# A forget gate in two passes, its norm amid the query product, and low key parts written once: one change to a two-block fp32 model kernel

## The chip, the cores and the metric

The kernel runs on one core of a Trainium2 chip. The metric is the device time of one execution in microseconds.

## What is computed

Two model blocks, one after the other, on 512 tokens of width 1024 in fp32. The first block has a gated linear recurrent layer and a "fox" attention layer; the second has two hybrid layers (short convolution, retention, MLP). The change lies in the fox layer, cut here to what matters:

```python
def rms_norm(x, g):
    y = xf * lax.rsqrt(jnp.mean(xf * xf, axis=-1, keepdims=True) + EPS)
    return (y * g.astype(jnp.float32)).astype(x.dtype)

def fox_mixer(h, w_in, b_f, w_out):          # 16 heads of 64
    u = h @ w_in
    q, k, v, gate = four times 1024 columns of u
    f_logit = u[..., 4 * FOX_WIDTH:] + b_f   # the last 16 columns, one for each head
    cum = jnp.cumsum(jax.nn.log_sigmoid(f_logit), axis=1)
    ...
        logits = jnp.einsum("bqhd,bkhd->bhqk", q_blk, kf) * scale
        logits = logits + (cq_blk[..., :, None] - ck[:, :, None, :])   # from cum
        logits = jnp.where(mask, logits, NEG_INF)
        p = jax.nn.softmax(logits, axis=-1)
        return jnp.einsum("bhqk,bkhd->bqhd", p, vf)
    ...
    return (o * jax.nn.silu(gate)) @ w_out
```

## The kernel before

Everything lies transposed, features on the 128 partitions and the 512 tokens on the free axis: `x` is 8 tiles of 128x512. TensorE multiplies in fp32r, a rounded fp32, and accuracy is had by splitting every operand into a rounded high part and a low part that holds the remainder. A product is three passes: high weights times high activations, high times low, low times high. The weights come from memory in chunks of 128x1024 (two tiles of 128x512). `w_raw`, `w_hi` and `w_lo` are rings of four chunks. For each chunk, three ahead of its use, ScalarE rounds `w_raw` to `w_hi` (`round_ahead`, L1271), VectorE subtracts to make `w_lo` (`remainder`, L1894), and TensorE waits for `lo_ready` before it uses the chunk.

The eight PSUM banks form two sets of four; products take them in turn ("turns"). A full product of four chunks is 96 matmuls: for each of 8 tiles of the contraction, four banks, three passes (L846, L847, L848; for v, where tokens come out on the partitions, L841 to L843). VectorE evacuates the four banks and multiplies by `rms`, one over the norm of each token: the norm's factor is applied behind the product, so `h` in the product is only `x` times the gain.

`schedule()` writes out the order of the work as a list of steps, and each engine walks the same list and does its own part of each step. In every step an engine first makes the chunks that it is due (`split_ahead`), then waits until the step before it is done (`join`), then does the step's own work (`statistics` first, where the step has it). A step may be opened and closed: its product is cut in two, and other steps stand between.

Around the change the order is this. The last residual product of the recurrent layer comes in two turns (`last_product`), and behind each turn stands a `norm` step for four of the eight tiles of `x`: ScalarE makes `h_hi` (L1518) and the square (L1563), VectorE `h_lo` (L2062) and the running sum of the squares `sumsq` (L2073), in turn, tile by tile. Then comes `forget`, a product with one chunk and one output bank:

```python
for k in range(DT):
    h_ready(k)
```

with three matmuls for each tile (L1049 to L1051). Its 128 weight columns hold the 16 forget columns four times over, at columns 0, 32, 64 and 96. Behind it, `statistics` (L947) sums `sumsq` over the partitions by one fp32 matmul with ones into the fourth bank of the same set; ScalarE takes the root (L1473), VectorE the reciprocal (L1967) and four reductions that lay `rms` out by token (L1973); then `forget` on VectorE reads from each 32-row group of the bank the tokens of one of four blocks and multiplies by `rms` (L2232).

The heads are handled in two halves of eight. Half 0 runs the steps `fq`, `log_sig`, `fk` opened, `cumulate`, `fk` closed, then `heads`: `v` opened, `first_head`, `v` closed, `attention` and the output gate. `log_sig` is a chain of 14 dependent small operations of VectorE (L2248 to L2260) with an exp on ScalarE amid them. `cumulate` makes the running sums. `fq` evacuates q (L2289) and stores for each head both parts stacked, 64 rows of high part (ScalarE, L1636) and 64 rows of low part (VectorE, L2294), in `q_parts`. `fk` stores `k_hi` (ScalarE, L1644) and `k_lo` (VectorE, L2303) twice each, in the upper and in the lower 64 rows. The scores of a head and a block of 128 query tokens are then two matmuls over all 128 rows:

```python
pe.matmul(bank[t][:, 0:n], q_parts[:, hh, q_cols], k_hi[:, hh, 0:n], start=True, stop=False)
pe.matmul(bank[t][:, 0:n], q_parts[:, hh, q_cols], k_lo[:, hh, 0:n], start=False, stop=False)
```

(L1073 and L1074; `n` is 128, 256, 384 or 512), followed by two bf16 matmuls that add the forget term (L1077) and the mask (L1079). In the `attention` step, for each head, TensorE makes the scores of the next one, values of a pair of heads (L1100, with 64 columns of weights, two heads side by side in the array), and the ten transposes of the probabilities (L1092).

## Time and profile before

| | |
|---|---|
| time, median of 3 runs | 2098.79 us (2098.56 to 2098.98) |
| span of the profiled execution, first to last instruction | 2097.1 us |
| mean granted clock of TensorE | 0.997 |
| TensorE busy | 2074.6 us, 99% |
| VectorE busy | 1564.8 us, 75% |
| ScalarE busy | 1067.8 us, 51% |
| GpSimd busy | 27.3 us, 1% |
| fox layer, forget product to the second half's gate | about 218 to 460 us of the span |

The span is of one profiled execution, whose own time beyond its span is not given apart; the times of the first line are of other executions of the same program. The ends of matmuls are modelled, so the distance from start to start says how long one takes, not the duration. "Idle before" in brackets is how long the engine stood idle and what ended it.

### The profile page before, as it was taken

How to read it: one execution, taken by the hardware profiler on the slowest of the kernel's cores; microseconds unless marked ns; L12 is line 12 of the kernel's file. 1: busy time of each engine (PE TensorE's matmuls, PEld its weight loads, DVE VectorE, ACT ScalarE, POOL GpSimd, SP SyncE). 2: the span in 40 equal slices, each digit the busy share in tenths (PEclk: the TensorE clock that was granted, in tenths of full speed). 3: DMA queues.
4: the chain of work that ended last, by engine and by line, in shares of the span. 5: the costliest groups of instructions: out<-in, count | busy, mean ns of one | idle time of the engine just before them, and what ended most of it. 6: DMA issues, size and time to landing. Idle time of an engine off the chain costs nothing.

```text
span 2097.1 us, 30779 instructions
## 1 busy us (share of the span) xinstructions
PE 2074.6 (99%) x12382; PEld 1869.8 (89%) x12382; DVE 1564.8 (75%) x2113; ACT 1067.8 (51%) x1522; POOL 27.3 (1%) x36
## 2 busy tenths in 40 slices
PE   9999999999999999999999999999999999999998
PEld 8888878878888899988999998888899988999997
DVE  8787785768656778866878887756778866868884
ACT  5776474646434445524555654434445534555653
POOL 0000000000000000000000000000000000000000
PEclk9999999999999999999999999999999999999999
DMA  5332222212322234432434353322234432344352
GB/s 186 111 101 100 91 81 71 91 66 84 107 85 87 81 111 136 146 111 91 121 107 118 118 162 105 107 91 81 91 101 141 145 107 91 121 115 118 114 175 83
DMA packets 63870, 227.96 MB, mean 109 GB/s; under 512 B 7216, under 2 KB 7600, under 8 KB 63600
## 3 DMA queue, kind: packets, MB, share of 16 engines
q1 hardware_dynamic: 59040, 208.83, 29.8%
q0 software_dynamic: 4544, 17.04, 4.7%
q8 instruction: 99, 1.62, 0.3%
q14 instruction: 43, 0.35, 0.1%
q10 hardware_dynamic: 144, 0.12, 0.0%
HBM read 223.86 MB, written 2.10 MB: 108 GB/s over the span
## 4 chain that ended last, share of the span: by engine, by line
PE 83%; DVE 3%; ACT 1%; issue 1%; DVEq 0%; ACTq 0%
PE bank L846 15%; PE bank L848 15%; PE bank L847 15%; PE bank L891 9%; PE bank L895 9%; PE bank L893 9%; PE bank L841 2%; PE bank L842 2%; PE bank L843 2%; PE bank L1100 1%; PE bank L1092 1%; ACT arena L1676 0%; PE bank L1169 0%; PE bank L1170 0%; PE bank L1168 0%
## 5 line engine op out<-in xcount | busy, mean ns | idle before, releaser
L1894 DVE TENSOR_TENSOR w_lo<-w_raw,w_hi 128x1024 fp32r<-128x1024 f32 x477 | 572.3, 1216 | 370.9 <-ACT w_hi L1271 368.9
L1271 ACT ACTIVATE w_hi<-w_raw 128x1024 fp32r<-128x1024 f32 x477 | 490.9, 1047 | 513.8 <-PE bank L848 333.1
L846 PE MATMUL bank<-h_both,w_hi 128*128 128x512 f32 x956 | 365.2, 382 | 2.0 <-DVE arena L1940 1.1
L847 PE MATMUL bank<-h_both,w_hi 128*128 128x512 f32 x956 | 362.3, 379 | 0.0
L848 PE MATMUL bank<-h_both,w_lo 128*128 128x512 f32 x956 | 362.3, 379 | 0.0
L846 PE MATMUL bank<-y_hi,w_hi 128*128 128x512 f32 x920 | 351.1, 382 | 5.4 <-DVE y_lo L1945 3.4
L848 PE MATMUL bank<-y_hi,w_lo 128*128 128x512 f32 x920 | 349.4, 380 | 0.0
L847 PE MATMUL bank<-y_lo,w_hi 128*128 128x512 f32 x920 | 349.2, 380 | 0.0
L846 PEld LDWEIGHTS bank<-h_both,w_hi 128*128 128x128 f32 x956 | 180.7, 189 | 30.1 <-issue 3.5
L847 PEld LDWEIGHTS bank<-h_both,w_hi 128*128 128x128 f32 x956 | 180.7, 189 | 25.9 <-issue 1.0
L848 PEld LDWEIGHTS bank<-h_both,w_lo 128*128 128x128 f32 x956 | 180.7, 189 | 25.6
L846 PEld LDWEIGHTS bank<-y_hi,w_hi 128*128 128x128 f32 x920 | 174.3, 190 | 31.8 <-DVE w_lo L1894 4.5
L847 PEld LDWEIGHTS bank<-y_lo,w_hi 128*128 128x128 f32 x920 | 174.4, 190 | 25.1 <-issue 0.7
L848 PEld LDWEIGHTS bank<-y_hi,w_lo 128*128 128x128 f32 x920 | 174.2, 189 | 24.8
L893 PE MATMUL bank<-h_both,w_hi 128*128 128x256 f32 x656 | 180.4, 275 | 0.0
L895 PE MATMUL bank<-h_both,w_lo 128*128 128x256 f32 x656 | 180.4, 275 | 0.0
L891 PE MATMUL bank<-h_both,w_hi 128*128 128x256 f32 x656 | 180.4, 275 | 0.0
L891 PE MATMUL bank<-y_hi,w_hi 128*128 128x256 f32 x512 | 141.2, 276 | 0.0
L893 PE MATMUL bank<-y_lo,w_hi 128*128 128x256 f32 x512 | 140.8, 275 | 0.0
L895 PE MATMUL bank<-y_hi,w_lo 128*128 128x256 f32 x512 | 140.8, 275 | 0.0
L891 PEld LDWEIGHTS bank<-h_both,w_hi 128*128 128x128 f32 x656 | 125.9, 192 | 0.2
L893 PEld LDWEIGHTS bank<-h_both,w_hi 128*128 128x128 f32 x656 | 125.9, 192 | 0.2
(340 smaller groups left out, 3624.9 us busy)
## 6 DMA issues: line engine op xcount, KB each, us to landing
w_raw<-in_stream SPq DMA_DIRECT2D x389, 512.0 KB, 3.6
w_raw<-in_stream POOLq DMA_DIRECT2D x30, 512.0 KB, 5.4
x<-in_x_t SPq DMA_DIRECT2D x8, 256.0 KB, 6.7
out_t<-x SPq DMA_DIRECT2D x8, 256.0 KB, 2.1
arena<-in_consts POOLq DMA_DIRECT2D x1, 1024.0 KB, 5.2
w_raw<-in_stream SPq DMA_DIRECT2D x2, 256.0 KB, 4.3
arena<-in_positions POOLq DMA_DIRECT2D x1, 256.0 KB, 6.0
vec_t<-in_vecs ACTq DMA_DIRECT2D x1, 112.5 KB, 3.2
```

The costliest lines, as they stand in the source:

```text
L841: pe.matmul(out, a_h[:, t], w_h, start=first, stop=False)
L842: pe.matmul(out, a_h[:, t], w_l, start=False, stop=False)
L843: mm = pe.matmul(out, a_l[:, t], w_h, start=False, stop=last)
L846: pe.matmul(out, w_hi[:, slot, w], streamed(a_h), start=first, stop=False)
L847: pe.matmul(out, w_hi[:, slot, w], streamed(a_l), start=False, stop=False)
L848: mm = pe.matmul(out, w_lo[:, slot, w], streamed(a_h), start=False, stop=last)
L891: pe.matmul(out, w_hi[:, slot, w], tokens(tile(0, k)), start=begin, stop=False, skip_group_check=True)
L893: pe.matmul(out, w_hi[:, slot, w], tokens(tile(1, k)), start=False, stop=False, skip_group_check=True)
L895: mm = pe.matmul(out, w_lo[:, slot, w], tokens(tile(0, k)), start=False, stop=end, skip_group_check=True)
L1092: mm = pe.transpose(turned_bank(j)[:, (t - j) * P:(t - j) * P + P], probs[:, hh % 2, at:at + P], ident[:, :])
L1271: A.activation(w_hi[:, slot, w], w_raw[:, chunks.raw_slot[raw], w], ACT.Copy).then_inc(hi_ready, 1)
L1894: V.tensor_tensor(w_lo[:, slot, w], src[:, w], w_hi[:, slot, w].bitcast(F32), ALU.subtract).then_inc(lo_ready, 1)
```

## The change

The forget weights hold the 16 forget columns once, at columns 0 to 15. Once the chunk is rounded, VectorE writes its low part into columns 32 to 47 of the same high chunk instead of into `w_lo`, so that one matmul carries high and low weights side by side and rows 32 to 47 of the output hold the low-weight product. The product then has two passes (with `h_hi` and with `h_lo`). The step `forget` has neither statistics nor an evacuation. `fq` of half 0 is opened with one chunk; then the new step `forget_rows` does the statistics matmul, root, reciprocal and reductions, and reads the forget bank by eight row operations: four of the low rows, four of the high rows. `log_sig` follows it and adds the two in its first operation; then `fq` is closed with its other three chunks. In the second `norm` step before the forget product, ScalarE makes its four `h_hi` first and then the four squares, and VectorE its four `h_lo` first and then the four sums. `k_lo` is written once for a head, in the rows where the high part of q lies, and the second scores matmul runs over these 64 rows alone.

```diff
@@ -151,10 +151,10 @@
     "residual": {},
-    "forget": {},
+    "forget": {}, "forget_rows": {"vec": TT},
     "log_sig": {"act_out": 1, "vec": 14},
     "cumulate": {"act_out": HEADS, "vec": 9 + TT + PARTS},
-    "fq": {"act_out": 8, "vec": 8}, "fk": {"act_out": 16, "vec": 16}, "v": {},
+    "fq": {"act_out": 8, "vec": 8}, "fk": {"act_out": 16, "vec": 8}, "v": {},
     "first_head": {}, "attention": {}, "last_turn": {}, "last_head": {},
...
@@ -259,8 +259,9 @@
              s("fox_gate", 2, 1, part="close", done=2)]
-    fox = [s("forget", 1, 1, True),
-           Bind("half", 0, [s("fq", 4, 1), s("log_sig"), *open_and_close("fk", s("cumulate")), *heads]),
+    fox = [s("forget", 1, 1),
+           Bind("half", 0, [s("fq", 1, 0, part="open", done=0), s("forget_rows", stats=True), s("log_sig"),
+                            s("fq", 3, 1, part="close", done=1), *open_and_close("fk", s("cumulate")), *heads]),
            Bind("half", 1, [s("fq", 4, 1), s("fk", 4, 1), *heads]),
...
@@ -939,11 +942,12 @@
-            def statistics(set_):
+            def statistics(set_, beside_forget=False):
 
                 pe.wait_ge(vec, T.mark["sumsq"])
 
-                wait(pe, evacuated, T.value("turn", 0, 4))
+                if not beside_forget:
+                    wait(pe, evacuated, T.value("turn", 0, 4))
                 pe.matmul(bank[set_ + 3][:, :], ones[:, :], sumsq[:, :], start=True, stop=True)\
...
@@ -1047,11 +1051,12 @@
                     pe.matmul(out, w_hi[:, slot, w], streamed(h_hi[:, k, :]), start=k == 0, stop=False)
-                    pe.matmul(out, w_hi[:, slot, w], streamed(h_lo[:, k, :]), start=False, stop=False)
-                    mm = pe.matmul(out, w_lo[:, slot, w], streamed(h_hi[:, k, :]), start=False, stop=k == DT - 1)
+                    mm = pe.matmul(out, w_hi[:, slot, w], streamed(h_lo[:, k, :]), start=False, stop=k == DT - 1)
                 mm.then_inc(bank_ready, 4)
 
-                statistics(set_)
+            def forget_rows(step):
+                statistics(4 - 4 * (T.fixed["turn"] % 2), beside_forget=True)
+                T.fresh_stats = True
...
@@ -1063,7 +1068,8 @@
-                    pe.wait_ge(vec, T.value("vec", 2 * (hh + 1) - HEADS))
+                    pe.wait_ge(vec, T.value("vec", hh + 1 - HEADS // 2))
+                    own = slice(HD, P) if hh % 2 else slice(0, HD)
                     for t in range(TT):
...
@@ -1071,7 +1077,7 @@
                         pe.matmul(bank[t][:, 0:n], q_parts[:, hh, q_cols], k_hi[:, hh, 0:n], start=True, stop=False)
-                        pe.matmul(bank[t][:, 0:n], q_parts[:, hh, q_cols], k_lo[:, hh, 0:n], start=False, stop=False)
+                        pe.matmul(bank[t][:, 0:n], q_parts[own, hh, q_cols], k_lo[own, hh, 0:n], start=False, stop=False)
                     for t in range(TT):
...
@@ -1466,8 +1472,7 @@
                 set_ = 4 * (T.fixed["turn"] % 2)
-                if step.kind != "forget":
-                    set_ = 4 - set_
+                set_ = 4 - set_
                 folded = step.kind == "qk" and T.var("layer") == 0
...
@@ -1517,7 +1522,11 @@
                         .then_inc(a_hi, 1)
-                    square(k, i)
+                    if step.args["part"] == 0:
+                        square(k, i)
+                if step.args["part"] == 1:
+                    for i in range(DT // 2):
+                        square(DT // 2 + i, i)
...
@@ -1891,6 +1900,11 @@
                 dve.wait_ge(hi_ready, T.value("chunk", n + 1))
+                if T.fixed["chunk"] + n in side_by_side:
+                    whole, rounded = (t.rearrange("p (k m) -> p k m", k=DT) for t in (src, w_hi[:, slot, :]))
+                    V.tensor_tensor(rounded[:, :, 32:32 + HEADS], whole[:, :, 0:HEADS], rounded[:, :, 0:HEADS].bitcast(F32),
+                                    ALU.subtract).then_inc(lo_ready, 1)
+                    return
                 V.tensor_tensor(w_lo[:, slot, w], src[:, w], w_hi[:, slot, w].bitcast(F32),
...
@@ -2086,7 +2100,11 @@
                     lo_of_h(k, i, gain_column(step, k))
-                    add_square(k, i + 1, i)
+                    if step.args["part"] == 0:
+                        add_square(k, i + 1, i)
+                if step.args["part"] == 1:
+                    for i in range(DT // 2):
+                        add_square(DT // 2 + i, i + 1, i)
...
@@ -2225,12 +2243,16 @@
             def forget(step):
-                banks(3)
-                for g in range(TT):
-                    rows, cols = slice(32 * g, 32 * g + 32), slice(P * g, P * g + P)
-                    of_group = product_bank(0)[rows, g // 2, g % 2 * P:g % 2 * P + P]
-                    V.tensor_tensor(quarter(0)[rows, :], of_group, rms[rows, cols], ALU.mult)\
-                        .then_inc(evacuated, 1)
+                pass
+
+            def forget_rows(step):
+                bank_of_forget = in_order(bank[4 - 4 * (T.fixed["turn"] % 2)][:, :])
+                for part, done in ((1, vec), (0, evacuated)):
+                    rows = slice(32 * part, 32 * part + 32)
+                    for g in range(TT):
+                        to, cols = slice(32 * g, 32 * g + 32), slice(P * g, P * g + P)
+                        of_group = bank_of_forget[rows, g // 2, g % 2 * P:g % 2 * P + P]
+                        V.tensor_tensor(quarter(part)[to, :], of_group, rms[rows, cols], ALU.mult).then_inc(done, 1)
...
@@ -2245,7 +2267,7 @@
                 f0, f1, f2, f3 = (quarter(n) for n in range(4))
-                link(V.tensor_scalar(f0, f0, vec_t[:, V_BF:V_BF + 1], None, ALU.add))
+                link(V.scalar_tensor_tensor(out=f0, in0=f0, scalar=vec_t[:, V_BF:V_BF + 1], in1=f1, op0=ALU.add, op1=ALU.add))
                 link(V.scalar_tensor_tensor(out=f1, in0=f0, scalar=-1.0, in1=f0, op0=ALU.mult, op1=ALU.max))
...
@@ -2299,9 +2321,8 @@
                     acted(2 * hh + 2)
-                    for to in (rows, other):
-                        V.tensor_tensor(k_lo[to, hh, :], fk[rows, hh // 2, :], k_hi[rows, hh, :].bitcast(F32),
-                                        ALU.subtract).then_inc(vec, 1)
+                    V.tensor_tensor(k_lo[rows, hh, :], fk[rows, hh // 2, :], k_hi[rows, hh, :].bitcast(F32),
+                                    ALU.subtract).then_inc(vec, 1)
...
@@ -2898,8 +2921,7 @@
             w = np.zeros((D, P), fox_w_in.dtype)
-            for g in range(TT):
-                w[:, 32 * g:32 * g + HEADS] = fox_w_in[:, 4 * D:]
+            w[:, 0:HEADS] = fox_w_in[:, 4 * D:]
             out.append(w.reshape(DT, P, P).transpose(1, 0, 2).reshape(1, P, CW))
```

`side_by_side` holds the index of the forget chunk. The steps' counts of semaphore increments change with them.

## Rows read from the trace of the kernel before

**Rows 1.** The page, part 1: busy time, share of the span, instructions.
```profile
PE 2074.6 (99%) x12382; PEld 1869.8 (89%) x12382; DVE 1564.8 (75%) x2113; ACT 1067.8 (51%) x1522; POOL 27.3 (1%) x36
```

**Rows 2.** Waits of TensorE, 205 to 500 us: total, times, longest.
```profile
PE bank L1049 <- DVE h_both L2062: 1.8, 4, 0.7
PE bank L841 <- DVE w_lo L1894: 1.7, 1, 1.7
```

**Rows 3.** Timeline of TensorE, forget product: start, duration, idle before in brackets.
```profile
218.45 0.38 PE L1049 MATMUL bank<-h_both,w_hi 128*128 128x512 f32 x1
...
220.82 0.38 PE L1051 MATMUL bank<-h_both,w_lo 128*128 128x512 f32 x1
221.94 0.48 PE L1049 MATMUL bank<-h_both,w_hi 128*128 128x512 f32 x1 [0.73 <-DVE h_both L2062]
...
226.48 1.02 PE L947 MATMUL bank<-sumsq,ones 128*128 128x512 f32 x2
...
227.56 0.38 PE L847 MATMUL bank<-h_both,w_hi 128*128 128x512 f32 x1
```

**Rows 4.** Timeline of VectorE, from the last residual to the key product.
```profile
218.73 2.49 DVE L2159 TENSOR_TENSOR x<-bank,x 128x512 f32<-128x512 f32 x4
221.12 0.76 DVE L2062 SCALAR_TENSOR_TENSOR h_both<-x,vec_t,h_both 128x512 fp32r<-128x512 f32 x1
221.78 0.70 DVE L2073 TENSOR_TENSOR sumsq<-sumsq,arena 128x512 f32<-128x512 f32 x1
...
228.44 3.35 DVE L1967 RECIPROCAL rms<-rms 128x512 f32<-128x512 f32 x1 [1.03 <-ACT rms L1473]
...
233.17 1.24 DVE L2232 TENSOR_TENSOR arena<-bank,rms 32x128 f32<-32x128 f32 x4
...
246.43 2.53 DVE L2289 SCALAR_TENSOR_TENSOR arena<-bank,rms 128x512 f32<-128x512 f32 x4 [1.03 <-PE bank L848]
...
254.79 0.29 DVE L2248 TENSOR_SCALAR arena<-arena,vec_t 128x128 f32<-128x128 f32 x1
...
261.59 2.36 DVE L1894 TENSOR_TENSOR w_lo<-w_raw,w_hi 128x1024 fp32r<-128x1024 f32 x2
```

**Rows 5.** Timelines of ScalarE and VectorE, parts of the keys, half 0.
```profile
273.98 10.43 ACT L1644 ACTIVATE y_hi<-arena 64x512 fp32r<-64x512 f32 x16 [5.65 <-DVE arena L1940]
...
275.57 11.44 DVE L2303 TENSOR_TENSOR y_lo<-arena,y_hi 64x512 fp32r<-64x512 f32 x16
```

**Rows 6.** Timeline of TensorE, v product and first heads, half 0.
```profile
288.32 0.48 PE L841 MATMUL bank<-w_hi,h_both 128*128 128x512 f32 x1 [1.73 <-DVE w_lo L1894]
...
293.61 0.23 PE L1073 MATMUL bank<-y_hi,q_parts 128*128 128x128 f32 x1
...
306.22 1.31 PE L1092 MATMUL bank<-ident,arena 128*128 128x128 f32 x10
```

**Rows 7.** Timeline of TensorE, first heads, half 1.
```profile
415.08 0.23 PE L1073 MATMUL bank<-y_hi,q_parts 128*128 128x128 f32 x1
...
417.09 0.22 PE L1079 MATMUL bank<-mask_b,ident_b 128*128 128x128 bf16 x1
417.14 1.26 PE L1092 MATMUL bank<-ident,arena 128*128 128x128 f32 x10
...
424.65 0.22 PE L1079 MATMUL bank<-mask_b,ident_b 128*128 128x128 bf16 x1
424.80 0.64 PE L1100 MATMUL bank<-arena 128*64 128x512 f32 x1
...
426.45 1.31 PE L1092 MATMUL bank<-ident,arena 128*128 128x128 f32 x10
```

**Rows 8.** Instructions of line 1074: duration ns min/median/max, starts, shapes.
```profile
L1074 PE MATMUL bank<-y_lo,q_parts x64: 272/307/398, 279.2 to 441.8; 128*128 128x128 f32 x16, 128*128 128x256 f32 x16, 128*128 128x384 f32 x16, 128*128 128x512 f32 x16
```

**Rows 9.** Timeline of TensorE, last values of half 0 and what follows.
```profile
326.06 0.39 PE L1100 MATMUL bank<-arena 128*64 128x128 f32 x4
326.38 0.48 PE L846 MATMUL bank<-h_both,w_hi 128*128 128x512 f32 x1
```

More of the change, by code:

```diff
@@ L180 @@
 STATS = {"stats": 1, "sumsq_read": 1, "vec": 1}
-TOKEN_COLUMNS = ("forget", "qk")
+TOKEN_COLUMNS = ("forget_rows", "qk")
 def schedule():
@@ L197, in s @@
             incs = {"act_out": DT // 2, "vec": 2}
-        if kind == "fox_gate" and args["part"] == "open":
+        if args.get("part") == "open":
             incs = {}
@@ L420, in build @@
     chunks = Chunks(steps)
-    half_filled, first_chunk = set(), 0
+    half_filled, side_by_side, first_chunk = set(), set(), 0
     for item in steps:
@@ L424, in build @@
             half_filled.add(first_chunk)
+        if isinstance(item, Step) and item.kind == "forget":
+            side_by_side.add(first_chunk)
         first_chunk += delta(item)["chunk"]
@@ L1212, in _ @@
             kinds = {"prep": prep, "norm": norm, "x": of_h, "gates": gates, "lru_gate": of_h,
-                     "residual": of_y, "forget": forget, "fq": of_h, "fk": of_h, "v": of_h,
+                     "residual": of_y, "forget": forget, "forget_rows": forget_rows, "fq": of_h, "fk": of_h, "v": of_h,
                      "first_head": attention, "attention": attention, "last_turn": attention,
@@ L1451, in join @@
             def join(step):
-                late = step.args.get("beside") or step.kind in ("taps", "norm", "squares", "fold", "final")
+                late = step.args.get("beside") or step.kind in ("taps", "norm", "squares", "fold", "final", "forget_rows")
                 if T.fixed["turn"] == 0 and step.kind == "norm":
@@ L1835, in _ @@
                      "taps": taps, "conv": conv, "input_gate": input_gate, "squares": squares,
-                     "forget": forget, "log_sig": log_sig, "cumulate": cumulate, "residual": residual,
+                     "forget": forget, "forget_rows": forget, "log_sig": log_sig, "cumulate": cumulate, "residual": residual,
                      "first_head": attention, "attention": attention, "last_turn": attention,
@@ L1904, in join @@
             def join(step):
-                late = step.args.get("beside") or step.kind in ("taps", "norm", "squares", "fold", "final")
+                late = step.args.get("beside") or step.kind in ("taps", "norm", "squares", "fold", "final", "forget_rows")
                 if T.fixed["turn"] > 0:
@@ L2811, in _ @@
             kinds = {"prep": prep, "norm": norm, "x": x_step, "lru_gate": lru_gate,
-                     "residual": residual, "forget": forget, "log_sig": log_sig, "cumulate": cumulate, "fq": fq_step,
+                     "residual": residual, "forget": forget, "forget_rows": forget_rows, "log_sig": log_sig, "cumulate": cumulate, "fq": fq_step,
                      "fk": fk_step,
@@ L2873, in order_of_weights @@
         rows = {"open": slice(0, D // 2), "close": slice(D // 2, D)}.get(args.get("part"))
+        if kind == "fq" and "done" in args:
+            rows = (slice(0, D // 4), slice(D // 4, D))[args["done"]]
         if kind == "fox_gate":
```

## The prediction

> **What bounds the kernel now.** I read the busy times of the page first. TensorE is busy for 2074.6 us, 99% of the span [rows 1]: time comes only from matmuls taken away or from a wait of TensorE taken away, and anything put on VectorE or ScalarE costs nothing as long as TensorE does not come to wait for it. I then read the waits of TensorE in the fox layer. Two matter: four short ones for `h_lo` in the forget product (L1049), and one of 1.7 us for the low part of a weight chunk in the v product (L841) [rows 2]. Then the timelines around both. A 512-column matmul starts every 0.2157 us (218.45 to 220.82 is eleven of them). The forget product is 24 matmuls, 5.18 us, but lasts from 218.45 to 226.48, 8.03 us: 2.85 us of it is waiting [rows 3].
>
> **A. The forget product and the order of the norm.** One of three passes goes: 8 x 0.2157 = 1.73 us less on TensorE. The wait shrinks too. VectorE now makes one `h_lo` in about 1.26 us (from 221.94 to 226.48 TensorE gets four tiles, the last of which takes 0.75), because an addition of squares stands between two of them; the `h_lo` alone have a pitch of 0.66 us (221.12 to 221.78) [rows 4]. It also reaches the first one earlier: the low split of the forget chunk, two splits ahead of the previous half's additions, handles 8 x 16 elements of a partition instead of 1024. Its nearest rows are the 128x128 operation at 254.79 (0.29 us, pitch about 0.3) and the full split (1.14 us per chunk where two run together) [rows 4]. I take the first, since time there goes with elements, so 0.85 us less; the upper bound is the full split, no gain. The additions at 218.73 start without idle time behind the splits, so VectorE sets them, and the banks are there for an earlier start: each bank's last three matmuls take 0.65 us and the product ends at 218.45, so the first bank is ready near 216.7. All of it moves from 218.73 to 217.9. The four `h_lo` then start at 220.27, 220.93, 221.59 and 222.25. TensorE started 0.82 us after the start of each (221.12 to 221.94), so the last tile starts at 223.07 and its two passes, with one uncovered weight load of 0.10 (the 0.48 of that row against 0.38), end at 223.61. The product lasts 5.16 us instead of 8.03: **-2.87 us**, of which 1.73 are passes and 1.14 wait. ScalarE's four `h_hi` have a pitch of about 0.65 and stay ahead. The squares that are now added last end at about 225.7, and nothing waits for them: the statistics matmul now stands behind a chunk of the query product, 24 matmuls, at 228.79.
>
> **B. The statistics amid the query product.** The fp32 matmul costs the same 0.86 us (226.48 to 227.56 less one pitch) [rows 3], only later. What follows it on VectorE is the risk: reciprocal, four `rms_col` reductions, now eight row operations instead of four, then the whole `log_sig` chain, and only behind these the low split of the first chunk of the key product. The splits of the last two query chunks are made before, at about 226 to 228.2, so those are safe. Counted from the start of the statistics matmul: reciprocal at +1.96 (228.44 less 226.48), row operations at +6.69 (233.17), eight of them 2.5 (1.24 for four), `log_sig` 6.8 (254.79 to 261.59; it holds a table load and an exp of ScalarE, which has nothing else then), the split 1.22 and 0.06 until TensorE starts: +17.3 [rows 3, 4]. TensorE arrives at +0.86 + 72 x 0.2157 = +16.39. So a new wait of **+0.9 us** appears at the first matmul of the key product. Behind it the same engine splits two more chunks and evacuates q; the banks of q are next needed by v, some 20 us later, so no second wait grows from it. If the eight row operations took half a microsecond each instead of 0.31, the wait would be 2.4 us; if they overlapped fully, it would still be 0.4. The bias and the sum of the two rows are one operation, as before.
>
> **C. Low part of the keys once.** VectorE does 8 subtractions instead of 16 in each half. Before, ScalarE's 16 `k_hi` ran from 273.98 for 10.43 us and VectorE's 16 `k_lo` from 275.57 to 287.0 [rows 5]; the next split came behind them, and TensorE waited for it until 288.32 [rows 6]. Afterwards ScalarE sets the pace (two `k_hi`, 1.3 us, for one `k_lo` of 0.69), so the last low part comes about 0.8 us after the last high part. Moreover the 6.8 us of `log_sig` no longer stand ahead of the evacuation of the keys; `log_sig` is over at about 244.8, three splits take 3.4, evacuation and low parts of q 8.4 (246.43 to 254.79), and what lies between the end of `log_sig` and the first `k_lo` 14.0 (261.59 to 275.57) [rows 4, 5]: first `k_lo` at 270.6. ScalarE's 16 then end near 279.3 and the low split near 281.5. In pitches the wait is 2.0 us: the 1.73 of the row, 0.16 by which the matmul before is modelled longer than a pitch (0.38 against 0.2157), and an uncovered load of 0.10. Without it, and with TensorE 1.95 us earlier by A and B, the split is needed at 284.5 (the 24 matmuls end at 293.61 today, so they began at 288.43). So **-2.0 us**. Were the `k_lo` only 2 us earlier, the split would end near 284.4, still in time.
>
> **D. Start of attention in half 0.** From the first scores matmul behind v to the transposes behind the first values, half 0 takes 293.61 to 306.22, 12.61 us [rows 6]. Half 1 runs the same instructions in 415.08 to 426.45, 11.37 us [rows 7], since there VectorE and ScalarE are not late from k and v. With C the first half should look like the second: **-1.2 us** (bounds: 0 and -1.3). Half 1 itself has no TensorE wait to lose and gains nothing from its eight subtractions.
>
> **E. The second scores pass over 64 rows.** 64 matmuls (L1074) [rows 8] now contract over 64 partitions instead of 128. The columns that stream are the same, so I expect no gain from that; below nothing, where the load of weights is the limit (16 matmuls of 128 columns), a shorter load could give at most 16 x 0.05 = 0.8 us. No row of this trace contracts over 64 partitions. The nearest are the value matmuls (L1100), which use 64 columns of the array. Where the shape stays 128x128, the engine goes on 0.05 us after L1079 (417.09 to 417.14); where it becomes 128x64, only 0.15 us after it (424.65 to 424.80) [rows 7]. On the way back, four matmuls of 128 columns (two side by side, 0.21 us of streaming at 0.05 a pass) are followed by L846 after 0.32 us, so 0.11 later, and that matmul shows an uncovered load (0.48 against 0.38) [rows 9]. A change of shape thus costs 0.10 + 0.10 going in and 0.11 + 0.10 coming back; about 0.36 us for each L1074, since for the narrow ones the load is partly uncovered today. The two ends are 0 and 64 x 0.36 = 23 us. I take 0, without much confidence: those rows show a change in how many columns are in use, which alters where weights and results go, and in E they stay as they are.
>
> The Trainium skill, page TensorEngine Tiling (Array Packing), section Tiling Modes, says that changing the tiling mode drains TensorE, and it counts 64x128 as a mode of its own. By that rule the sum would take the 23 us; the trace agrees for 128x64 [rows 7, 9] and shows nothing for 64 rows.
>
> **The sum.** -2.87 + 0.9 - 2.0 - 1.2 + 0 = -5.2 us. The profiled span is 2097.1 us and the median of the three times 2098.79, 1.7 us outside the span that nothing here touches: 2093.6 us.
>
> **Rivals.**
> 1. *Every switch to 64 rows and back is paid.* Place: scores of all 16 heads. Price 64 x 0.36 = 23 us, of which I let 2 us fall into waits that the first heads of a half have anyway (D shows 1.2 us of such slack in one half). Time: 2098.8 - 5.2 + 21 = 2114.6 us, slower by 0.75%. For it: the two measured shape changes. Against it: those are changes of columns. It decides from about 0.08 us a matmul, where it eats the whole gain; from 0.15 the kernel is slower beyond the bound below. If only the pauses are paid and the loads stay covered, 64 x 0.21 = 13 us: 2107.
> 2. *No switch cost, but the gains do not add up.* The wait at the first key chunk is longer (a row operation slower than 0.31, a join of semaphores), the strided split is no shorter (0.85 lost), or D stays away (1.2 lost): 2094.5 to 2096.5 us. For it: the chain in B is serial, every delay in it goes to TensorE. Against: each link has its own row.
>
> **How the numbers follow.** A measurement of this kernel tells about 0.2%, 4.2 us, from no change. Forecast (2092 to 2094.6): 0.46, nearly all of it faster. Rival 2: 0.16, mostly within 0.2%. Rival 1: 0.33 in full, near 2115, and 0.05 in part, near 2103 to 2107. Faster 0.45, same 0.16, slower 0.39. Range 2092.0 to 2117.0: below lies only a cheaper load in E, above only a switch dearer than its rows; the forecast's own range is 2092.0 to 2095.0.
>
> **What would show it.** A: L1049 to the statistics or next product 5.2 us, three waits of about 0.2 us. B: a wait near 0.9 us of L846 for `w_lo` at the first key chunk, and L1473 about 1.1 us after a statistics matmul that starts near 228.8. C: no wait at L841. D: 11.4 us from scores to transposes in both halves. E: the passes of L1073 and L1074 of a head as long as before; in rival 1 each weight load of L1074 starts only behind the matmul ahead of it, and those passes take 1.4 us more a head (4 x 0.36). The prediction is wrong if the heads late in a half get longer, or if the wait in B is over 2 us.

## The result and the profile after

The changed kernel takes 2114.66 us (median of 4 runs, 2114.0 to 2115.89) where the kernel before takes 2098.89 (median of 4): ratio 1.0074, 95% interval 1.0062 to 1.0086. It is slower by 15.8 us, 0.75%. The forecast was 2093.6.

The page of the changed kernel, part 1 (answers to [rows 1]):

```profile
PE 2091.4 (99%) x12364; PEld 1874.0 (89%) x12374; DVE 1555.3 (74%) x2101; ACT 1068.6 (51%) x1522; POOL 27.3 (1%) x36
```

TensorE is busy 16.8 us longer, though the change takes eight matmuls away (the counts differ by 18 because some records are missing). The waits of TensorE in the fox layer, 205 to 520 us (answers to [rows 2]; line numbers have moved: L1053 is the forget product, L849 the first pass of a product):

```profile
PE bank L849 <- DVE w_lo L1908: 0.8, 1, 0.8
PE bank L1053 <- DVE h_both L2076: 0.7, 1, 0.7
```

The wait at the v product is gone and one at the first key chunk has come. The timeline of TensorE at the forget product (answers to [rows 3]), then at the end of the query product:

```profile
219.97 0.38 PE L1053 MATMUL bank<-h_both,w_hi 128*128 128x512 f32 x1
...
224.81 0.38 PE L1054 MATMUL bank<-h_both,w_hi 128*128 128x512 f32 x1
...
230.21 1.02 PE L951 MATMUL bank<-sumsq,ones 128*128 128x512 f32 x2
```

```profile
246.39 0.38 PE L851 MATMUL bank<-h_both,w_lo 128*128 128x512 f32 x1
247.56 0.48 PE L849 MATMUL bank<-h_both,w_hi 128*128 128x512 f32 x1 [0.79 <-DVE w_lo L1908]
```

The forget product starts at 219.97, 1.5 us later than before, mostly for a reason outside the change. In the recurrent layer TensorE waits 3.4 us for a low part of activations, in every kernel here, and goes on near 162; what the clock does behind this wait differs between executions. The windows from 160 to 170 us of the kernel before and of the changed kernel (the third figure from the end is the granted clock):

```profile
160.00:170.00 10.00, 7.72 (x28) 6.53 (x29) 6.84 (x9) 7.70 (x13) 0.00 (x0) 0.83 0.29 101
160.00:170.00 10.00, 7.24 (x21) 5.99 (x22) 6.36 (x8) 8.12 (x12) 0.00 (x0) 0.66 0.27 85
```

So 1.7 us of full speed were lost there before, and 3.4 us in the profiled execution of the changed kernel. From its first matmul to the first of the query product behind it, which starts 0.22 after 224.81, are 5.06 us instead of 8.03. The statistics matmul stands behind 24 matmuls of the query product. The timeline of VectorE in this part (answers to [rows 4, 5]):

```profile
209.66 0.28 DVE L1905 TENSOR_TENSOR w_hi<-w_raw,w_hi 128x128 fp32r<-128x128 f32 x1
...
221.72 2.72 DVE L2076 SCALAR_TENSOR_TENSOR h_both<-x,vec_t,h_both 128x512 fp32r<-128x512 f32 x4
...
246.28 3.49 DVE L1908 TENSOR_TENSOR w_lo<-w_raw,w_hi 128x1024 fp32r<-128x1024 f32 x3
...
280.78 0.69 DVE L2324 TENSOR_TENSOR y_lo<-arena,y_hi 64x512 fp32r<-64x512 f32 x1 [0.62 <-ACT y_hi L1653]
281.86 2.36 DVE L1908 TENSOR_TENSOR w_lo<-w_raw,w_hi 128x1024 fp32r<-128x1024 f32 x2 [0.40 <-ACT w_hi L1277]
```

The forget chunk's low split takes 0.28 us (209.66), the four `h_lo` run together (2.72 for all), `log_sig` is done at 246.28 and only then come the splits for the keys, of which the first ends 1.2 us later: TensorE goes on at 247.56. The last `k_lo` (280.78) has waited 0.62 us for ScalarE's `k_hi`; it ends at 281.5, and the next split (1.2 of the 2.36 us from 281.86) at 283.1. The timeline of TensorE from the first scores matmul behind v to the transposes behind the first values (answers to [rows 6]):

```profile
292.58 0.22 PE L1079 MATMUL bank<-y_hi,q_parts 128*128 128x128 f32 x1
...
306.78 1.31 PE L1098 MATMUL bank<-ident,arena 128*128 128x128 f32 x10
```

14.20 us, where the forecast had 11.4. The cause is in the scores. One head later in half 0, the timeline of TensorE, L1079 over 128 rows and L1080 over 64:

```profile
319.62 0.31 PE L1079 MATMUL bank<-y_hi,q_parts 128*128 128x128 f32 x1
319.86 0.32 PE L1080 MATMUL bank<-y_lo,q_parts 64*128 64x128 f32 x1
...
321.48 0.50 PE L1079 MATMUL bank<-y_hi,q_parts 128*128 128x512 f32 x1
321.91 0.50 PE L1080 MATMUL bank<-y_lo,q_parts 64*128 64x512 f32 x1
322.34 0.23 PE L1083 MATMUL bank<-arena 128*128 128x128 bf16 x1
```

and the weight loads of the last two of these:

```profile
321.48 0.19 PEld L1079 LDWEIGHTS bank<-y_hi,q_parts 128*128 128x128 f32 x1 [0.19 <-issue]
321.91 0.18 PEld L1080 LDWEIGHTS bank<-y_lo,q_parts 64*128 64x128 f32 x1 [0.24 <-issue]
```

From the first of the scores matmuls to the first bf16 one (L1083) are 2.72 us. The 512-column pair takes 0.43 us a matmul (321.48 to 321.91 to 322.34), of which 0.216 is streaming: the load of L1080 begins at 321.91, that is 0.11 behind the end of the streaming of L1079 (321.48, load 0.10, streaming 0.22), and then another 0.10 passes until it is in. The same happens in both directions. Only the sum, 0.43 less 0.216, is read directly here: 0.10 for the load is by how much the rows of matmuls with an uncovered load exceed 0.38 (0.48 at 247.56), while the load's own row says 0.18. e9 below shows the pause by itself. The extra of a pair of matmuls over e1 below depends on the columns: by the starts of this head and of the same head in e1, the pairs of 128, 256, 384 and 512 columns take 0.49, 0.62, 0.75 and 0.86 us where they take 0.25, 0.29, 0.35 and 0.47, so 0.24, 0.33, 0.40 and 0.39 more.

To compare executions, the stretch from the first forget matmul to the start of the last value matmul of half 1 is taken from the instructions of these two lines; what lies outside does the same work in all kernels. Over the twelve traces its first end varies by 2.3 us (217.7 to 220.0) and what is left of the span behind the stretch by 2.5 us (1636.7 to 1639.2).

| kernel | first forget matmul | last value matmul | stretch, us |
|---|---|---|---|
| before | 218.5 | 460.4 | 241.9 |
| changed | 220.0 | 475.9 | 255.9 |
| e1, low part twice, 128 rows | 218.5 | 455.3 | 236.8 |
| e2, zeros in the other rows, 128 rows | 218.8 | 455.9 | 237.1 |
| e3, 64-row matmuls grouped | 219.1 | 461.6 | 242.5 |
| e4, before with 64 rows | 217.7 | 476.2 | 258.5 |
| e5, e2 with q in three parts | 219.1 | 455.1 | 236.0 |
| e6, before with low parts first | 218.7 | 462.9 | 244.2 |
| e7, e1 with q in three parts | 219.9 | 456.7 | 236.8 |
| e8, e1 without the new order | 218.3 | 456.9 | 238.6 |
| e9, e1 with one 64-row matmul a head | 219.1 | 459.9 | 240.8 |
| e10, changed again | 218.1 | 474.1 | 256.0 |

The stretch of the changed kernel is 14.0 us longer than before (e10: 14.1), its time 15.8 us longer (e10: 15.1). The interval of the time, 13.0 to 18.0 us, holds both.

### The profile page after: what moved, and what is told of

Its sections match the earlier page's. It is cut to its first block, busy times and chain, and to the rows that moved or that the text cites. A ratio compares the mean times of both kernels' runs of the same rounds, so it can differ in the third digit from the quotient of the medians.

```text
span 2114.1 us, 30745 instructions
## 1 busy us (share of the span) xinstructions
PE 2091.4 (99%) x12364; PEld 1874.0 (89%) x12374; DVE 1555.3 (74%) x2101; ACT 1068.6 (51%) x1522; POOL 27.3 (1%) x36
## 4 chain that ended last, share of the span: by engine, by line
PE 88%; DVE 3%; issue 1%; ACT 1%; DVEq 0%; ACTq 0%
PE bank L849 16%; PE bank L850 16%; PE bank L851 16%; PE bank L894 9%; PE bank L896 9%; PE bank L898 9%; PE bank L844 2%; PE bank L846 2%; PE bank L845 2%; PE bank L1080 1%; PE bank L1106 1%; PE bank L1098 1%; PE bank L1079 1%; PE bank L1176 0%; PE bank L1175 0%
## 5 line engine op out<-in xcount | busy, mean ns | idle before, releaser
L849 PE MATMUL bank<-h_both,w_hi 128*128 128x512 f32 x956 | 365.3, 382 | 3.5 <-DVE h_both L2076 1.1
L849 PE MATMUL bank<-y_hi,w_hi 128*128 128x512 f32 x920 | 351.6, 382 | 5.4 <-DVE y_lo L1959 3.4
L849 PEld LDWEIGHTS bank<-h_both,w_hi 128*128 128x128 f32 x956 | 180.7, 189 | 31.9 <-issue 3.8
L849 PEld LDWEIGHTS bank<-y_hi,w_hi 128*128 128x128 f32 x920 | 174.6, 190 | 31.9 <-DVE w_lo L1908 4.5
## 6 DMA issues: line engine op xcount, KB each, us to landing
x<-in_x_t SPq DMA_DIRECT2D x8, 256.0 KB, 7.0
out_t<-x SPq DMA_DIRECT2D x8, 256.0 KB, 2.1
w_raw<-in_stream SPq DMA_DIRECT2D x2, 256.0 KB, 4.6
arena<-in_positions POOLq DMA_DIRECT2D x1, 256.0 KB, 6.0
```

Source lines behind the costliest of these rows:

```text
L849: pe.matmul(out, w_hi[:, slot, w], streamed(a_h), start=first, stop=False)
```

## Experiments

The ratios of e1 to e4 are to 2099.63 us of the kernel before, those of e5 and e6, on another chip, to 2098.98, and those of e7 to e10 to 2099.42.

**e1: the low part twice, scores over 128 rows.** The changed kernel with its last part undone:

```diff
-                    V.tensor_tensor(k_lo[rows, hh, :], fk[rows, hh // 2, :], k_hi[rows, hh, :].bitcast(F32),
-                                    ALU.subtract).then_inc(vec, 1)
+                    for to in (rows, other):
+                        V.tensor_tensor(k_lo[to, hh, :], fk[rows, hh // 2, :], k_hi[rows, hh, :].bitcast(F32),
+                                        ALU.subtract).then_inc(vec, 1)
...
-                        pe.matmul(bank[t][:, 0:n], q_parts[own, hh, q_cols], k_lo[own, hh, 0:n], start=False, stop=False)
+                        pe.matmul(bank[t][:, 0:n], q_parts[:, hh, q_cols], k_lo[:, hh, 0:n], start=False, stop=False)
```

> The changed kernel with one part undone: the low part of the keys is written twice again and the second scores matmul runs over 128 rows. Theory (the loss is all in the 64-row matmuls): the scores passes of a head fall from 2.64 to 1.28 us, 16 x 1.36 = 21.8 us come back, less 1 us that the 64 rows hid in waits of the first heads, and the time is about 2093.7. The eight more subtractions a half should not bring the wait at the v product back, because log_sig no longer stands ahead of them: a wait under 0.5 us there. Rival (the other parts lose as well): the time stays above 2098.9. Second rival (the halved k_lo work is what paid in the v product): the wait of about 2 us is back and the time is near 2096.

Measured: 2094.17 us, ratio to before 0.9975 (0.9966 to 0.9984); the stretch is 5.1 us shorter than before. All four other parts together pay what they should, and the whole loss hangs on the scores. The timelines of its scores, of the weight load of the last f32 one, and of TensorE from the scores behind v to the first values:

```profile
311.27 0.30 PE L1079 MATMUL bank<-y_hi,q_parts 128*128 128x128 f32 x1
...
312.16 0.40 PE L1079 MATMUL bank<-y_hi,q_parts 128*128 128x512 f32 x1
312.40 0.40 PE L1080 MATMUL bank<-y_lo,q_parts 128*128 128x512 f32 x1
312.63 0.23 PE L1083 MATMUL bank<-arena 128*128 128x128 bf16 x1
```

```profile
312.17 0.19 PEld L1080 LDWEIGHTS bank<-y_lo,q_parts 128*128 128x128 f32 x1
```

```profile
289.73 0.23 PE L1079 MATMUL bank<-y_hi,q_parts 128*128 128x128 f32 x1
...
299.49 0.64 PE L1106 MATMUL bank<-arena 128*64 128x512 f32 x1
...
301.14 1.31 PE L1098 MATMUL bank<-ident,arena 128*128 128x128 f32 x10
```

The passes take 1.36 us in the same place of a head where they took 2.72. The load for the matmul at 312.40 starts at 312.17, while the matmul ahead of it streams; in the changed kernel it started at 321.91 together with its own matmul. The stretch from v to the transposes is 11.41 us, as in half 1 before. VectorE's timeline at the keys:

```profile
270.44 11.44 DVE L2325 TENSOR_TENSOR y_lo<-arena,y_hi 64x512 fp32r<-64x512 f32 x16
281.91 2.36 DVE L1908 TENSOR_TENSOR w_lo<-w_raw,w_hi 128x1024 fp32r<-128x1024 f32 x2
```

With 16 subtractions it is done at 281.9 and the split that v needs is in at 283.1, 64.6 us after the first forget matmul; with eight it is in after 63.1. The v product begins 24 x 0.2157 before 289.73, at 284.55, without a pause: 1.4 us were to spare. So the halved subtractions were not what took that wait away; `log_sig` being ahead was enough, beside the other parts of the change. Both rivals fell. This is the version to keep: 0.25% faster than the kernel before.

**e2: written once, zeros in the other rows.** On the changed kernel; ScalarE writes the zeros ahead of q of half 0:

```diff
+                    for s, rows in enumerate((slice(HD, P), slice(0, HD))):
+                        A.activation(k_lo[rows, s::2, :], x[rows, 0:HEADS // 4, :], ACT.Copy, scale=0.0).then_inc(act_out, 1)
...
-                        pe.matmul(bank[t][:, 0:n], q_parts[own, hh, q_cols], k_lo[own, hh, 0:n], start=False, stop=False)
+                        pe.matmul(bank[t][:, 0:n], q_parts[:, hh, q_cols], k_lo[:, hh, 0:n], start=False, stop=False)
```

> The changed kernel, low part of the keys still written once, but ScalarE writes zeros into the other 64 rows once, in an idle stretch ahead of q of half 0, and the second scores matmul runs over all 128 rows. Same products as in the changed kernel. Theory (only the switches of shape cost): scores passes of a head 1.28 us, time about 2093.6, within 0.1% of the kernel with the low part written twice. Rival (the halved subtractions of VectorE are worth something of their own): at least 1.5 us below that kernel. Second rival (contracting over fewer rows was not the cost, the once written low part was): the time stays near 2114.

Measured: 2096.14 us, 0.9985 (0.9976 to 0.9994), stretch 237.1. With the low part still written once, 18.8 us of the stretch come back: contracting over 64 rows is the cost, not how the operand is made. It is 0.3 us longer than e1 in the stretch and 2.0 us in the median; the 0.3 lies in the first heads of half 0 (11.66 us from scores to transposes, 11.41 in e1), the second number is not explained by the trace and stays open, and the intervals of the two overlap. Both rivals fell.

**e3: the four 64-row matmuls of a head together.**

```diff
                         pe.matmul(bank[t][:, 0:n], q_parts[:, hh, q_cols], k_hi[:, hh, 0:n], start=True, stop=False)
+                    for t in range(TT):
+                        n = P * (t + 1)
+                        q_cols = slice(t * P, n)
                         pe.matmul(bank[t][:, 0:n], q_parts[own, hh, q_cols], k_lo[own, hh, 0:n], start=False, stop=False)
```

> The changed kernel with the same 64 matmuls over 64 rows, but the four of a head stand together behind the four over 128 rows, so there are two switches of shape a head instead of eight. Theory (a switch costs, not the 64-row matmul): the extra falls from 1.36 us a head to about 0.36, 16 x 1.0 = 16 us less than the changed kernel, time about 2099. Rival (a matmul over 64 rows is slow wherever it stands): still 2114.7, and the second to fourth of the 64-row matmuls start as late behind each other as now.

Measured: 2101.61 us, ratio 1.0011 (1.0002 to 1.002). The timeline of TensorE at a later head; L1083 here is the 64-row matmul and L1086 the bf16 one:

```profile
314.06 0.90 PE L1079 MATMUL bank<-y_hi,q_parts 128*128 128x128 f32 x4
314.88 0.90 PE L1083 MATMUL bank<-y_lo,q_parts 64*128 64x128 f32 x4
315.71 0.23 PE L1086 MATMUL bank<-arena 128*128 128x128 bf16 x1
```

The same 64 matmuls over 64 rows, 13 us faster than in the changed kernel. The passes take 1.65 us, 0.29 more than in e1 for two switches. Four matmuls over 64 rows take 0.83 us, as the four over 128 rows (0.82). So a matmul over 64 rows is not slow in itself, and the rival fell. Of the 5.7 us over e1, 16 x 0.29 = 4.6 are switches; TensorE also waited 0.9 us in all, in four waits, for exps, which its order now meets sooner. The time came out 2.6 us above what was expected.

**e4: the kernel before with 64 rows, nothing else.**

```diff
-                        pe.matmul(bank[t][:, 0:n], q_parts[:, hh, q_cols], k_lo[:, hh, 0:n], start=False, stop=False)
+                        pe.matmul(bank[t][:, 0:n], q_parts[own, hh, q_cols], k_lo[own, hh, 0:n], start=False, stop=False)
```

> The kernel before with one edit: the second scores matmul runs over 64 rows (the low part of the keys is still written twice). Theory (the whole loss is in this one edit): 16 x 1.36 = 21.8 us more, less about 2 us in all that fall into the waits at the v product of half 0 and in the first heads, time 2118 to 2120.7, so dearer than the whole change. Rival (the loss needs the other parts too, the new order of q and log_sig for one): under 2110.

Measured: 2115.61 us, 1.0081 (1.0065 to 1.0096), stretch 16.6 us longer. The one edit makes the loss. It is smaller than expected: of 21.8 us, 5.2 fall into waits instead of 2. The wait for the split at v shrank from 1.7 to 0.4 us, since the scores ahead of it are longer. The rest lies in the first heads: from scores to transposes are 14.18 and 14.20 us in the two halves where 12.61 and 11.37 were, while three heads at 1.36 more would make 4.1 more each.

**e5: q in one, one and two chunks.** On e2:

```diff
-            ... s("forget_rows", stats=True), s("log_sig"), s("fq", 3, 1, part="close", done=1, zero=True)
+            ... s("forget_rows", stats=True), s("fq", 1, 0, part="open", done=1), s("log_sig"),
+                s("fq", 2, 1, part="close", done=2, zero=True)
```

> The kernel with zeros in the other rows and 128-row scores, and one edit on top: the query product of half 0 is cut into 1, 1 and 2 chunks, and log_sig stands behind the second opening, so that the low split of the first key chunk is made by VectorE before the log_sig chain. Theory (the wait of 0.8 us at the first key chunk is VectorE's serial chain ahead of that split): the wait goes, log_sig ends 1.1 us later and nothing waits for that, time 0.8 us below the kernel with zeros alone, near 2092.8. Rival (the wait moves to the second key chunk or to the v product): same time as that kernel, with a new wait in the trace.

Measured: 2094.82 us, 0.9982 (0.9973 to 0.9991). The wait at the first key chunk is gone and the stretch is 1.1 us shorter than in e2. It was VectorE's chain. The medians of e5 and e2 come from different chips, and the difference is below what they can tell.

**e6: the new order of the norm step alone**, on the kernel before:

```diff
-                    square(k, i)
+                    if step.args["part"] == 0:
+                        square(k, i)
+                if step.args["part"] == 1:
+                    for i in range(DT // 2):
+                        square(DT // 2 + i, i)
```

and the same for `h_lo` and the sums on VectorE.

> The kernel before with one edit: in the norm step ahead of the forget product the four low parts of h come before the four sums of squares (and the four high parts before the squares). The forget product keeps three passes and the statistics matmul stands directly behind it. Theory (the order only pays because the statistics matmul moved away): the waits at the forget product shrink by 1.8 us, but the statistics matmul then waits for the last sum and starts at 226.5 to 226.7 as before; no change in time, 2098.9. Rival (the order pays by itself): 1.1 to 1.8 us less.

Measured: 2101.59 us, 1.0013 (1.0004 to 1.0022), stretch 2.3 us longer. Neither theory had it slower. Its wait for the statistics, ScalarE's third square, TensorE around the statistics matmul (L947), and two windows of 4 us (busy time of each engine; the third figure from the end is the granted clock):

```profile
PE bank L947 <- DVE sumsq L2077: 2.1, 1, 2.1
```

```profile
224.78 0.63 ACT L1567 ACTIVATE arena<-x 128x512 f32<-128x512 f32 x1 [1.36 <-DVE sumsq L2077]
```

```profile
224.74 0.38 PE L1051 MATMUL bank<-h_both,w_lo 128*128 128x512 f32 x1
227.19 1.12 PE L947 MATMUL bank<-sumsq,ones 128*128 128x512 f32 x2 [2.08 <-DVE sumsq L2077]
227.75 0.94 PE L846 MATMUL bank<-h_both,w_hi 128*128 128x512 f32 x1
228.48 0.63 PE L847 MATMUL bank<-h_both,w_hi 128*128 128x512 f32 x1
228.91 0.63 PE L848 MATMUL bank<-h_both,w_lo 128*128 128x512 f32 x1
```

```profile
227.00:231.00 4.00, 3.81 (x9) 2.75 (x10) 3.11 (x3) 1.79 (x3) 0.00 (x0) 0.66 0.38 119
231.00:235.00 4.00, 4.00 (x18) 3.46 (x17) 3.73 (x13) 0.00 (x0) 0.00 (x0) 0.92 0.03 12
```

The forget product is done sooner, but the last sum comes later than before: the squares have two buffers, so ScalarE's third square waits 1.36 us for VectorE's first sum, which now stands behind four low parts. TensorE waits 2.08 us, and then its matmuls are 0.43 us apart (228.48 to 228.91) instead of 0.216, at 1.2 GHz: the mean granted clock of the next four us is 0.66. The statistics matmul starts 0.5 us later after the first forget matmul than before (8.49 against 8.03), and the clock accounts for 1.7 us more: four us at 0.66 and four at 0.92 of full speed are 4 x 0.34 + 4 x 0.08. Together 2.1 of the 2.3. The part of the clock is read from one trace; the median of eleven executions, 2.6 us above the kernel before, agrees with the sum.

**e7: e1 with q in three parts.** The edit of e5 on e1, with the low part written twice.

> The kernel with the low part of the keys written twice and 128-row scores (e1), and the query product of half 0 in 1, 1 and 2 chunks with log_sig behind the second opening. The version that should beat both. Theory: in its trace the stretch from the first forget matmul to the last value matmul is 0.8 us shorter than in e1 (236.8 us), so 236.0; the time 0.8 us below e1, which is less than the interval. The rival (the key parts now come too late for v, since VectorE has 16 subtractions again behind a log_sig that is 1.1 us later): a wait of over 0.5 us at the v product and no gain over e1.

Measured: 2094.18 us, 0.9975 (0.9966 to 0.9984); stretch 236.8, the same as e1. The wait at the first key chunk is gone, but the first heads take longer. TensorE from the second head's scores to the first values:

```profile
290.09 0.23 PE L1080 MATMUL bank<-y_hi,q_parts 128*128 128x128 f32 x1
...
300.89 0.64 PE L1107 MATMUL bank<-arena 128*64 128x512 f32 x1
```

10.80 us, where e1 has 9.76 (289.73 to 299.49). VectorE and ScalarE are not later: counted from the first forget matmul, VectorE makes its first `k_lo` after 51.9 us and the first values start after 81.0 us, in e1 as in e7. TensorE comes to the second head's scores 1.1 us sooner (after 70.2 us instead of 71.2) and loses it there, since the two others set the pace of the first heads: the rival was right on the gain, not on the place. In e5, which makes 8 subtractions a half and not 16, the same cut of q keeps its 1.1 us, and its stretch is 0.8 us shorter than that of e7. So once `log_sig` is later, the halved work of VectorE does pay, by the traces; the times of e5 and e7 cannot tell it.

**e8: e1 with the old order of the norm step**, the edit of e6 taken back.

> e1 with the norm step in its old order (a square added between two low parts of h), so two forget passes and moved statistics without the new order. Theory: with a pitch of 1.27 us for a low part the last forget tile starts 1.8 us later, the forget product takes about 7.0 us instead of 5.1 and the time is 1.8 us above e1. Rival (with two passes the order no longer matters): same as e1.

Measured: 2095.74 us, 0.9986 (0.9977 to 0.9994), 1.6 us above e7; stretch 238.6, 1.8 us above e1. As expected: beside the moved statistics the order is worth 1.8 us, and without them (e6) it costs 2.3.

**e9: one 64-row matmul a head.** On e1, only the 512-column one:

```diff
+                        rows_of_low = own if t == TT - 1 else slice(0, P)
-                        pe.matmul(bank[t][:, 0:n], q_parts[:, hh, q_cols], k_lo[:, hh, 0:n], start=False, stop=False)
+                        pe.matmul(bank[t][:, 0:n], q_parts[rows_of_low, hh, q_cols], k_lo[rows_of_low, hh, 0:n], start=False, stop=False)
```

> e1 with one of the four low-part matmuls of a head (the one of 512 columns, in the middle of nothing but 128-row matmuls) over 64 rows. Two switches of shape a head, as in e3, but one 64-row matmul instead of four. Theory (what is paid is the switch): the scores passes grow by about 0.4 us a head, as in e3, 16 x 0.4 = 6.2 us above e1. Rival (the matmul over 64 rows is what costs): a quarter of e3's cost, 1.5 us.

Measured: 2097.35 us, 0.9991 (0.9982 to 1.0), 3.2 us above e7; stretch 4.0 above e1. Expected were 6.2, with 0.4 us a head; 0.29 was found, 4.6 us for 16 heads. The rival's 1.5 us is too small. The timeline of TensorE at a later head (L1081 is the low-part matmul, L1084 the bf16 one):

```profile
313.35 0.30 PE L1079 MATMUL bank<-y_hi,q_parts 128*128 128x128 f32 x1
...
314.25 0.40 PE L1079 MATMUL bank<-y_hi,q_parts 128*128 128x512 f32 x1
314.57 0.49 PE L1081 MATMUL bank<-y_lo,q_parts 64*128 64x512 f32 x1
315.00 0.23 PE L1084 MATMUL bank<-arena 128*128 128x128 bf16 x1
```

1.65 us again, to the hundredth what e3 takes with four such matmuls. What is paid is the switch, two for a head in both. The weight loads of the first bf16 matmul, in e1 and in e9, both start only with their own matmul:

```profile
312.63 0.10 PEld L1083 LDWEIGHTS bank<-arena 128*128 128x128 bf16 x1 [0.28 <-issue]
```

```profile
314.99 0.10 PEld L1084 LDWEIGHTS bank<-arena 128*128 128x128 bf16 x1 [0.24 <-issue]
```

So the load behind the 64-row matmul is no new cost here: what is new is the pause ahead of it, its own uncovered load and the pause behind it, 0.11 + 0.10 + 0.11, which come to 0.29 by the pitches (0.32 + 0.43 against 0.24 + 0.23 in e1, and 0.01 over the rest of the head). The pause can be read here without a load beside it: the matmul at 314.25 has its load covered and streams 0.216, yet the next starts 0.32 later.

**e10: the changed kernel again.**

> The changed kernel itself, beside e7 to e9 on the same chip, as their common measure. Both theories: 2114.7, and 19 us above e1's siblings, of which 19.1 lie between the first forget matmul and the last value matmul.

Measured: 2114.51 us, 1.0072 (1.0057 to 1.0088), stretch 256.0, and 20.3 us above e7, 1.3 more than expected.

## Why the prediction was wrong

The step that failed is E: it took 0 for the second scores pass, where its own upper end, 64 x 0.36 = 23 us, was nearly right. Measured are 2.72 - 1.36 = 1.36 us a head, 0.34 a matmul on average and 21.8 us in all, of which 19.1 reach the stretch (255.9 against e1's 236.8). The reason given for 0 was that the rows at hand change the columns in use and not the rows; e3 and e9 show that a change of rows is paid the same way, 0.11 of pause and 0.10 of uncovered load in each direction between f32 matmuls.

The sign that the prediction had named, heads late in a half getting longer, came. Rival 1 described this and gave 2114.6 us. That it meets the median to 0.1 us is luck: its 23 us were 21.8 and its 2 us of slack 2.7, which gives 2112.8, and the interval of the time is five us wide; the chance it had, 0.33, was too low, for the nearest rows [rows 7, 9] spoke for it and nothing in the trace against it. The Trainium skill, page TensorEngine Tiling (Array Packing), section Tiling Modes, has changes of mode drain the engine and names the 64-row mode among them; the trace agrees, with 0.11 us from the end of streaming to the next load.

- **A**, forecast -2.87: the product and its waits fell from 8.03 to 5.06, -2.97. Right within 0.1; e8 shows that 1.8 us of the stretch hang on the order of the norm step.
- **B**, forecast +0.9: the wait is 0.79 by the row and 0.96 in pitches (247.56 less 246.39 is 1.17, less 0.216). Right in place and size, and its cause is shown by e5 and e7, where it goes when one split is made ahead of `log_sig`.
- **C**, forecast -2.0: the wait is gone, but the step gave two causes and only one works. e1 makes 16 subtractions again and does not wait. The halved work of VectorE took no wait away at v; only with q in three parts is it worth 0.8 us of the stretch (e5 against e7).
- **D**, forecast -1.2: in e1 the first heads take 11.41 instead of 12.61, exactly that. In the changed kernel it cannot be read: its first heads take 14.20 us in both halves, but so they do in e4, which has no C.
- **Sum of A to D**, forecast -5.2: e1's stretch is 5.1 us shorter, and its ratio 0.9975 on 2098.8 gives 2093.6, with an interval of 2091.7 to 2095.4. Rival 2, gains that do not add up, fell with it in the stretch.

## What to carry to other kernels

Beside dense matmuls over 128 rows, each change to 64 rows and back cost 0.24 us where all matmuls alternated and had 128 columns, and up to 0.40 where they had more. One switch there and back in a head cost 0.29 us, as much for one 64-row matmul as for four together. So fill the other rows with zeros or a copy, or put all matmuls of one shape together. Where a cost has no row of its own but the nearest rows show a price, take that price unless the trace itself holds a reason against it. Where an edit removes a wait, ask which part of it did: the earlier `log_sig` was enough here, and the halved work of an engine that TensorE did not wait for was bought with the loss.

## What the runs showed of the hardware that was not expected

- TensorE's granted clock fell from 2.4 to 1.2 GHz behind a wait of 2.08 us in a dense stretch (e6; pitch 0.43 us instead of 0.216). The wait of 0.79 us in the changed kernel and the 1.73 us at v in the kernel before [rows 6] left the distance of the 512-column matmuls behind them at 0.216.
- The same wait was not always followed by the same clock: behind the 3.4 us wait near 162 us, in the same work of all twelve traces, 1.7 us of full speed were lost in seven, 3.4 us in three (the changed kernel, e7, e9) and nothing in two (e4, e8). The changed kernel itself lost 3.4 us there in one profiled execution and 1.7 us in the other (e10).
- Matmuls over 64 and over 128 rows of the same columns took the same time when they followed their own kind: 0.83 and 0.82 us for the four of a head (e3).
